# A recurrence of sixteen tiles: transposes by another engine, a shorter inverse, and a new written-out order

## The reference, cut to what matters

```python
def step(S, inp):
    r_t, w_t, k_t, v_t, kk_t, a_t = inp
    sa = einsum("bhvk,bhk->bhv", S, -kk_t)
    S = (S * w_t[:, :, None, :] + sa[..., None] * (kk_t * a_t)[:, :, None, :]
         + v_t[..., None] * k_t[:, :, None, :])
    o_t = einsum("bhvk,bhk->bhv", S, r_t)
    return S, o_t
...
o = ((o - mean) * rsqrt(var + LNX_EPS) * lnx_g + lnx_b)
o = o + sum(r * k * r_k, axis=-1, keepdims=True) * v
o = o.reshape(B, T, D) * silu(g)
return o @ w_o, h[:, -1], S
```

## Time and profile before

| what | value |
|---|---|
| median of 3 runs | 2031.78 us (2031.47 to 2036.8) |
| the profiled execution's own time | 2030.11 us |
| its span | 2028.4 us |
| recurrence, tiles' part (slots 1 to 16) | 522.9 to 877.3 us of the span |
| slot 17 and the woven output projection | 877.3 to 920.6 us |
| trunk | 920.6 us to the end |

### The profile page before, as it was taken

The page is one execution under the profiler, slowest core; times in us unless marked ns, Lnnn a source line. Parts: engine busy times, 40 slices in busy tenths (PEclk is TensorE's granted clock), DMA queues, the critical chain, the costliest instruction groups (busy, mean ns, idle before and its releaser), DMA issues.

```text
span 2028.4 us, 49604 instructions
## 1 busy us (share of the span) xinstructions
PE 1886.5 (93%) x20798; PEld 1623.7 (80%) x20798; DVE 1014.0 (50%) x1686; ACT 815.6 (40%) x1443; POOL 244.3 (12%) x308
## 2 busy tenths in 40 slices
PE   7999999999999999999999899999999999777797
PEld 7988999999888888879998677677777677343697
DVE  7744363634455556634544543443455444677344
ACT  4234232334455555523333333332333444655233
POOL 0200000000244444413200000000000000110032
PEclk9999999999999999989999999999999999999899
DMA  7545555544132322105488999999999999999541
GB/s 284 173 143 177 165 181 171 170 158 149 56 106 85 91 89 84 55 22 189 150 333 315 411 414 419 397 425 424 425 424 424 407 422 383 415 407 378 230 145 73
DMA packets 122959, 505.55 MB, mean 249 GB/s; under 512 B 16033, under 2 KB 55330, under 8 KB 77474
## 3 DMA queue, kind: packets, MB, share of 16 engines
q1 hardware_dynamic: 122754, 502.60, 64.9%
HBM read 470.24 MB, written 32.32 MB: 248 GB/s over the span
## 4 chain that ended last, share of the span: by engine, by line
PE 31%; DMA 16%; DVE 3%; ACT 2%; issue 2%; SPq 1%; DVEq 0%; ACTq 0%
DMA at_vraw<-in_cache_v 16%; PE psP L2566 8%; PE psP L2568 7%; PE psP L2567 7%; PE at_psO L2616 5%; PE at_psS L2595 3%; SPq L1979 1%; PE psP L2661 0%; PE at_psT L2607 0%; DVE wlo L2328 0%; SPq L2019 0%; DVE at_o_new L2483 0%; ACT at_p_w L2286 0%; ACT at_p_w L2284 0%; SPq L1997 0%
## 5 line engine op out<-in xcount | busy, mean ns | idle before, releaser
L2566 PE MATMUL psP<-xhi,whi 128*128 128x320 f32 x1488 | 477.6, 321 | 2.5 <-DVE xlo L2453 1.9
L2567 PE MATMUL psP<-xlo,whi 128*128 128x320 f32 x1488 | 462.3, 311 | 0.0
L2568 PE MATMUL psP<-xhi,wlo 128*128 128x320 f32 x1488 | 462.2, 311 | 0.0
L2566 PEld LDWEIGHTS psP<-xhi,whi 128*128 128x128 f32 x1488 | 282.0, 189 | 67.1 <-issue 66.4
L2328 DVE TENSOR_TENSOR wlo<-wraw,whi 128x2048 fp32r<-128x2048 f32 x92 | 212.9, 2315 | 209.0 <-ACT whi L2154 208.7
L2154 ACT ACTIVATE whi<-wraw 128x2048 fp32r<-128x2048 f32 x92 | 176.0, 1913 | 279.9 <-PE psP L2568 278.3
L2567 PEld LDWEIGHTS psP<-xlo,whi 128*128 128x128 f32 x1488 | 282.3, 190 | 0.1
L2568 PEld LDWEIGHTS psP<-xhi,wlo 128*128 128x128 f32 x1488 | 281.8, 189 | 0.0
L131 PE MATMUL psP<-xhi,whi 128*128 128x320 f32 x704 | 218.4, 310 | 2.8 <-DVE wlo L166 2.3
L132 PE MATMUL psP<-xlo,whi 128*128 128x320 f32 x704 | 217.8, 309 | 0.0
L133 PE MATMUL psP<-xhi,wlo 128*128 128x320 f32 x704 | 217.8, 309 | 0.0
(11 more groups left out here) (378 smaller groups left out, 3212.9 us busy)
## 6 DMA issues: line engine op xcount, KB each, us to landing
wraw<-in_weights SPq DMA_DIRECT2D x160, 1024.0 KB, 6.1
at_kraw<-in_cache_k SPq DMA_DIRECT2D x96, 1024.0 KB, 11.1
at_vraw<-in_cache_v SPq DMA_DIRECT2D x94, 1024.0 KB, 11.1
at_kraw<-in_cache_k SPq DMA_DIRECT2D x64, 512.0 KB, 9.5
at_vraw<-in_cache_v SPq DMA_DIRECT2D x62, 512.0 KB, 10.6
rw_s0t<-in_s0T SPq DMA_DIRECT2D x16, 256.0 KB, 3.1
o_wkv_s<-rw_SN SPq DMA_DIRECT2D x16, 256.0 KB, 2.3
resT<-in_xT SPq DMA_DIRECT2D x8, 320.0 KB, 5.1
```

Source lines behind the costliest of these rows:

```text
L2566: pe.matmul(out, wh, c_.xhi[:, kc, :], start=(kc == 0), stop=False)
L2567: pe.matmul(out, wh, c_.xlo[:, kc, :], start=False, stop=False)
L2568: last = pe.matmul(out, wl, c_.xhi[:, kc, :], start=False, stop=(kc == NM - 1))
```

## The change

1. DVE transposes blocks of 32x32 within the partitions of a quarter (`dve.transpose`). `Dt`, `D2t`, `Yt`, `Et` and a new `X1t` are made so; `Dt` and `D2t` are block diagonal in groups of 8, and the others are kept zero outside the two 32x32 blocks. The PE steps `Dt`, `D2t`, `Yt`, `Et` and their ACT copies go.
2. `Vn`, `Bn`, `Kn` are also transposed by DVE. For v, the tile is loaded a second time with its two off-diagonal blocks exchanged (four DMAs, `VS`). For `Bn`, `Kn` DVE transposes (`Bt`, `Kt`), ACT copies to `Bn`/`Kn`, and four DMAs each move the off-diagonal blocks across partitions (`move_blocks`, counted by `turned_in`).
3. The mask `mFI` keeps of E only what lies inside the blocks of 32. The doubling ends with `Z1`, `E2t`, `X`; the steps `E2`, `E4t`, `Z2` go. The upper right corner of the inverse comes from two products, 32 columns wide: `Ht` and `XB`.
4. `Ht`, `XB` and the closing norm of a tile (`LATE`) run one slot later; there is a slot 18. `OT` has two buffers.
5. The copies `U0` to `U3` and `U4` go from DVE to ACT. SP issues in the order of `AT`. `ORDER` is new. In slots 17 and 18 the output projection is woven after `XB`.

```diff
+class StepMarks:        # as Marks, with the tile and slot of each step
...
-F.a.sq F.a.ka1 R.t.U0 R.a.Q4 R.a.SA4 R.t.Q4 R.a.O0 P.t.AB R.t.SA0 R.g.Vnx R.v.U0 F.v.cs R.t.U4 P.t.s4 R.t.S0
...
+P.t.s4 F.a.sq P.t.Ht R.g.Vnx F.a.kk0 P.t.AB P.v.s3 P.a.Ht P.v.Bt P.v.D4s F.v.cs R.t.mean F.a.Pi F.g.csm P.v.D F.a.ka1
+R.t.U0 P.t.XB R.v.cen F.g.k2 R.t.Q4 P.v.Dt P.a.XB R.a.U0 P.v.KK P.a.Bn P.g.ID R.t.SA0 P.t.D2 R.a.Q4 R.v.SA0 R.a.csq
+P.v.FR R.t.S0 P.a.D2 R.t.U4 R.v.ST0 R.t.var P.a.A12 P.v.D2t R.a.U4 R.a.SP1 R.t.U1 P.v.Vn R.a.lnv R.t.SA4 P.t.W F.v.rk
+R.a.U1 R.a.SA4 F.a.Pc R.t.SA1 P.t.D4t R.a.rstd R.v.SA1 F.g.Rz P.v.W F.t.ss R.v.on P.a.D4t F.a.Pm R.t.S1 P.t.Y R.a.ong
+R.v.ST1 F.v.ssm R.t.U2 R.g.oy P.v.Y R.t.O1 F.a.ln F.t.bon R.a.U2 P.v.Yt R.a.SP2 R.g.SAx R.a.O1 F.a.rn R.t.SA2 P.t.E
+R.v.SA2 P.v.Kt R.t.S2 P.a.E R.t.SN R.v.ST2 P.a.Kn P.v.Et R.a.SP3 F.v.kk P.t.Z1 R.v.SNa F.g.ka R.t.U3 P.v.Z1 P.t.E2t
+R.a.U3 F.g.Kz F.v.Az R.t.O2 P.a.E2t R.t.SA3 R.t.O0 R.a.O2 R.g.y R.v.SA3 P.t.X F.v.Bz R.a.O0 R.t.O4 P.v.X R.g.SNb
+R.t.S3 R.a.O4 R.t.O3 P.v.X1t R.a.xh F.v.bonus R.a.O3 R.v.xl R.v.ST3
...
+LATE = set("""R.t.mean R.v.cen R.a.csq R.t.var R.a.lnv R.a.rstd R.v.on R.a.ong R.g.oy R.g.y R.a.xh R.v.xl P.t.Ht P.a.Ht
+P.t.XB P.a.XB""".split())
...
-    for slot in range(TILES + 2):
-        side_by_side(beside(slot), *[stage(t) for stage, t in ((front, slot), (products, slot - 1), (run, slot - 2))
-                                     if 0 <= t < TILES])
+    for slot in range(TILES + 3):
+        in_slot = ((front, slot, 0), (products, slot - 1, 0), (products, slot - 2, 1), (run, slot - 2, 0), (run, slot - 3, 1))
+        side_by_side(beside(slot), *[stage(t, late) for stage, t, late in in_slot if 0 <= t < TILES])
...
+    own = c_.mFI[:, 0].rearrange("p (i s) -> p i s", i=2)
+    made(pool.tensor_tensor(own, own, c_.side[:].unsqueeze(2).to_broadcast([P, 2, HL]), ALU.mult))
...
+            def load_blocks_of_v(t):
+                for h in range(2):
+                    for a_ in range(2):
+                        q = L * h + HL * a_
+                        src = spilled("v", t)[L * h:L * h + L].rearrange("(b q) (c a s) -> q c b a s", b=2, a=2, s=HL)
+                        sp.dma_start(VS[q:q + HL], src[:, :, :, a_]).then_inc(vs_in, 16)
+            def move_blocks(x, turned):
+                for h in range(2):
+                    for a_ in range(2):
+                        q, o = L * h + HL * a_, L * h + HL * (1 - a_)
+                        sp.dma_start(x[q:q + HL, :, HL * (1 - a_):HL * (1 - a_) + HL],
+                                     turned[o:o + HL, :, a_]).then_inc(turned_in, 16)
...
+                    elif name == "Bt":
+                        F.v.wait(dve, "Bz", t)
+                        if t:
+                            dve.wait_ge(turned_in, 128 * t)
+                        Q.v.done(dve.transpose(BT[:].rearrange("p c b s -> p (c b s)"), flat(BZ[t % 2][:])), name)
+                    elif name == "D2t":
+                        Q.a.wait(dve, "D2", t)
+                        Q.v.done(dve.transpose(flat(D2t[:]), flat(D2[:])), name)
+                    elif name == "X1t":
+                        Q.v.wait(dve, "X", t)
+                        Q.v.done(dve.transpose(flat(Xt), flat(X[t % 2][:, 0:NCH])), name)
...
                     elif name == "D2":
-                        Q.a.wait(pe, "Dt", t)
-                        Q.t.done(each(ps, Dt, D, CH), name)
-                    elif name == "D2t":
-                        Q.a.wait(pe, "Dt", t)
-                        Q.t.done(each(ps, D, Dt, CH), name)
+                        Q.v.wait(pe, "Dt", t)
+                        Q.t.done(each(ps, all_of(Dt), all_of(D)), name)
...
+                    elif name == "Ht":
+                        Q.a.wait(pe, "A12", t)
+                        Q.v.wait(pe, "X1t", t)
+                        Q.t.done(each(ps, all_of(A12), all_of(Xt), HL), name)
+                    elif name == "XB":
+                        Q.a.wait(pe, "Ht", t)
+                        Q.v.wait(pe, "X", t)
+                        Q.t.done(each(ps, all_of(Ht), all_of(X[j][:, 0:NCH, HL:L]), HL), name)
...
                         elif name[0:2] == "SA":
                             if c == 0:
-                                Q.v.wait(pe, "X", t)
-                            R.v.wait(pe, f"U{c}", t)
+                                Q.a.wait(pe, "XB", t)
+                            R.a.wait(pe, f"U{c}", t)
...
                         elif name[0] == "S":
                             if c == 0:
-                                Q.a.wait(pe, "Bn", t)
-                                Q.a.wait(pe, "Kn", t)
+                                pe.wait_ge(turned_in, 128 * (t + 1))
```

More of the change, by code:

```diff
@@ L320, in done, with __init__, wait, last @@
         ins.then_inc(self.sem, 1)
+class StepMarks:
+    def __init__(self, sem, stage, engine):
+        self.sem, self.seen = sem, 0
+        self.turns = [(x, slot - behind(f"{stage}.{engine}.{x}")) for slot in range(TILES + 1)
+                      for x in steps_of(stage, engine) if 0 <= slot - behind(f"{stage}.{engine}.{x}") < TILES]
+        self.count = {turn: k + 1 for k, turn in enumerate(self.turns)}
+    def wait(self, eng, name, it):
+        eng.wait_ge(self.sem, self.count[name, it])
+    def last(self, *names):
+        return max(names, key=lambda x: self.count[x, 0])
+    def done(self, ins, name):
+        assert self.turns[self.seen][0] == name, name
+        self.seen += 1
+        ins.then_inc(self.sem, 1)
 HS = 64
@@ L419, in of, with before @@
         return self.turns.index(name) % self.n
-    def before(self, name):
+    def before(self, name, t):
         first, out = self.turns.index(name), []
         for k in range(first, first + self.turns.count(name)):
-            held = [j for j in range(len(self.turns)) if j % self.n == k % self.n]
-            out.append((self.turns[held[held.index(k) - 1]], held[0] != k))
+            held = [x for j, x in enumerate(self.turns) if j % self.n == k % self.n]
+            slot, i = t + behind(f"{self.stage}.t.{name}"), k // self.n
+            while slot >= 0:
+                slot, i = (slot, i - 1) if i else (slot - 1, len(held) - 1)
+                tile = slot - behind(f"{self.stage}.t.{held[i]}")
+                if slot >= 0 and 0 <= tile < TILES:
+                    out.append((held[i], tile))
+                    break
         return out
@@ L1211, in front, with products @@
                                                 bias=less_ka[:, t:t + 1]), name)
-            def products(t):
-                into = {"Vn": Vn[t % 2], "Bn": Bn[t % 2], "Kn": Kn[t % 2], "Dt": Dt, "D2": D2, "D2t": D2t,
-                        "D4t": D4t, "Yt": Yt, "E": E, "Et": Et, "E2": D2, "E2t": D2t, "E4t": D4t}
-                for name in steps_of("P", "a"):
+            def products(t, late):
+                into = {"D2": D2[:], "D4t": D4t[:], "E": E, "E2t": E2t}
+                a_part = psP[:, banks_p.of("AB")].rearrange("p (c x l) -> p c x l", c=NCH, l=L)[:, :, 0]
+                for name in steps_of("P", "a", late):
@@ L1224, in run @@
+            def run(t, late):
+                if t == 0 and not late:
                     act.wait_ge(c_.stored, g_stored)
-                for name in steps_of("R", "a"):
+                for name in steps_of("R", "a", late):
                     yield AT["R.a." + name]
@@ L1553, in products @@
+                        Q.t.done(each(ps, all_of(D2), all_of(D2t)), name)
                     elif name == "Y":
@@ L1605, in run @@
                 rb = [FR[j][:, c, 1] for c in range(NCH)] + [S3[j][:, 0]]
-                for name in steps_of("R", "t"):
+                for name in steps_of("R", "t", late):
                     yield AT["R.t." + name]
```

516 lines of the change are left out of this document (284 added, 232 removed), and 4 rows, old and new, of the table READ_BY.

## The result

The changed kernel took 1963.9 us (median of 4 runs, 1958.6 to 1972.9); the kernel before took 2031.7 beside it. The ratio is 0.9679, with a 95% interval of 0.9645 to 0.9714. The forecast was 1967.

What follows compares the result with a forecast made beforehand. PE's own instruction list was taken to bound the recurrence. Savings of 60.5 (fourteen slots) + 2.5 + 4.3 - 3 = 64.3 us from 2030.1 give 1965.8, plus 1.7 for the median: 1967; range 1948 to 1996.

Steps and rivals of the forecast that it cites:

- PE's list: Full slots of the recurrence: PE's own instructions set the length; 74 calls at 0.0583 us go, saving 4.32 us a slot.
- I let them cancel: Full slots: fewer "issue" stalls against copies waiting oftener behind DVE transposes, taken as equal, leaving 18.06 us a slot.
- Narrow steps: Ht and XB on PE: 16 calls of 32 columns each, at the full price of 64-column calls.
- DVE: Full slots: transposes at 0.485 us (320 columns) and 0.425 (256), making DVE 15.2 us busy a slot.
- Rival A: Full slots: DVE becomes the bound, transposes near 0.8 us, slots about 20 us, 35 us saved, time 1997; chance 0.12.
- ACT and POOL: Full slots: ACT goes from 12.8 to about 12.1 us, POOL stays at 9.4 us, both below PE.
- Slot 1: First slot of the recurrence, bound by the chain of products: 2.5 us saved.
- The tail: End of the recurrence: slot 16 saves 4.3 us, slots 17 and 18 together lose 3 us.
- used it only as a rival: Recurrence slots: gaps bring PE to half clock, slots of 26.0 us, time about 2080, slower than before; chance 0.03.
- The moves and SP: Full slots: SP's 21 issues at 0.33 us take 7 of 18 us; moves land within 4 us cover, costing nothing.

Runs made afterwards that it cites:

- the second chip: The changed kernel run once more, unchanged, as partner of the next kernels on the same chip: 1961.2 us (median of 6), slot 17.92 us.
- that of the norm: Changed kernel with the closing norm back in its tile's own slot, its steps at the end of every engine's list in a plain order: 2079.6 us.
- the first trace: Profile of the changed kernel from its first measurement, nothing altered: this execution took 1958.6 us, slot 18.17 us.

## Why the prediction came out right, step by step

- **PE's list.** The slot was forecast at 18.06 and is 18.17 (17.92 on the second chip). The calls alone bring 3.5 of the 4.3 us, and the slot is 0.7 to 1.0 us shorter beyond that. The step "I let them cancel" hit the sum by two errors of about 0.8 us each, which is in part luck: the list counts in full only when no wait lies in the slot.
- **Narrow steps.** 0.44 us each, priced 0.47: right.
- **DVE.** Transposes near 0.50 and 0.45 us; 211.99/14 = 15.1 us in a slot, 15.2 forecast. The nearest-row value held; the estimate from the Trainium skill ("VectorE: DVE Perf Modes", The three transpose paths; 0.51 for 320 columns) is closer still, and the trace agrees with it. Rival A fell on its price; whether a DVE that is 83% full costs the slot anything is open (0.23 us for 0.8 us more of copies, within chance). Two operations changed price by their neighbours: `Az` went from 492 ns to the 1130 above, and xlo from 493 to 670 (the row is of the kernel before, same view). POOL worked beside `Az` in both orders. By the trace its `ka` began 45 ns behind `Az` in the old one; in the new one its `Kz` begins 75 ns before `Az` and ends 0.79 us into it, just as it lay over `Bz` in the old order. In these rows it is the operation that finds POOL already at work that is long.

```profile
L1334 DVE SCALAR_TENSOR_TENSOR rw_AR<-rw_kk,rw_pm 128x320 f32<-128x320 f32 x14 | 6.9, 492 | 0.5
```

- **ACT and POOL.** 11.7 and 9.3 us, 12.1 and 9.4 forecast.
- **Slot 1.** 2.3 saved, 2.5 forecast. The old slot 1 was 16.96 us in the warm-up profile, not 18.22, so by that pair it is 1.0.
- **The tail.** This is the mis-sized term. I counted -3 for slots 17 and 18 and +4.3 for slot 16, 1.3 together; it was 8.9. Of this 5.6 us is the half clock of the profiled execution before, which another old tail did not have; at full clock on both sides the tail saved about 3.2 us (60.6 to 57.4). So most of the miss, 5.6 of 7.6 us, lies in which execution was profiled, and 2.0 in my pricing. I had seen the drop and used it only as a rival. Whether the change makes it rarer is open: it fell in two of three old tails and in one of nine new ones (the changed kernel's two profiles and its variants, without that of the norm). The last pause ahead of the woven products is 1.29 us in the old and 0.90 in the new.
- **The moves and SP.** Priced at nothing, and they cost 0.2 us or nothing. They landed in 2.3 to 2.4 us (median; 1.5 taken from the earlier trace rows). But SP's issue was mis-sized by half (0.64 to 0.97 us for many short runs), so the queue stood at 13 us and not 7. What I left out is who else uses it: four weight loads make four slots 1.9 us longer than the others, 7.6 us in all. In the kernel before the same loads made them 1.1 us longer, 4.5 in all, so against it the term left out is some 3 us. In slot 4 of the first trace the row shows both parts, PE standing and then half clock (0.58):

```profile
574.97:595.88 20.91, 18.61 (x432) 16.34 (x428) 15.04 (x37) 12.27 (x39) 9.39 (x11) 0.92 0.47 132
583.00:586.00 3.00, 0.85 (x19) 0.61 (x17) 0.34 (x1) 1.24 (x3) 1.43 (x2) 1.00 0.59 113
586.00:589.00 3.00, 3.00 (x52) 2.48 (x48) 1.52 (x4) 1.58 (x5) 0.00 (x0) 0.58 0.29 73
```

What PE waits for in such a slot the profile calls "issue". Removing the load from the slot removed the wait, and the packets' times say that it is PE's own instructions, late behind the load; that was not shown by a run of its own.

Not tried: all eight transposes without the corner and the norm's move, and the old placing of the norm under a planned order, since that needs the planner. So the parts of the change aren't priced one by one; that two transposes alone, in the old order, brought 6 us (1 to 11) of the 15 that their calls were worth (18 x 0.0583 x 14) is shown.

## What to carry to other kernels

When PE's list sets the time, a removed call is worth its full time only until the next wait shows. Put idle calls back into the new kernel to see how much of the gain is the calls and how much slack remains. A list ordered by hand or by a planner can be full of steps that cover a wait: taking some out without a new order brought half of their worth here, or nothing. And where the profile shows half clock beside the change, look at a second execution of the same order first: a forecast against one profiled execution takes that execution's stalls for the kernel's.

## What the runs showed of the hardware

- A VectorE transpose of 32 x 32 blocks of four-byte values took 0.47 to 0.51 us for 320 columns and 0.43 to 0.45 for 256, about as much as an addition or product of that width (0.49 and 0.41).
- SP needed 0.64 to 0.97 us to issue a transfer made of 128-byte runs (means of four), and up to 5.9 us for four when 4 MB lay ahead. The load of a, in long rows, took 0.32 us in the old kernel, 0.82 on average behind the moves of `Kn` and 0.33 with the moves left out.
- Beside a load of 1 MB a 16 KB block on the queue of instructions came 6.8 to 8.1 us behind the one before it, 5.2 on average, and PE stood still for 1.4 to 2.2 us until some 1.5 us after it had landed.
- PE fell to half clock in slots where it had stood 2 us (0.85 us busy of 3.00, row above) or 5.5 us of 25. Behind one and the same pause of 1.29 us in the old tail it fell twice and kept its clock once.
- A DVE operation of 320 columns with three operands took 492 ns when it began before POOL's and 1130 when POOL's instruction was already running, as long as `Bz` took before.
